# Opening of a two-layer diffusion backbone: filters of both layers in pairs, tokens in two-tile loads, low operands last

## The reference

```
per layer:
  ada = silu(cond) @ w_ada + b_ada          -> sh1, sc1, g1, sh2, sc2, g2
  h   = x * (1 + sc1) + sh1
  z   = h @ w_in                            (1024 x 2816: Hyena, Conformer, q, k, v)
  Hyena filter, for each length L in (1024, 256), from weights alone:
    feats = [t, cos, -sin]                  (L x 33)
    hid = sin(freq * (feats @ w1 + b1)); hid = sin(freq * (hid @ w2 + b2))
    hf  = hid @ w3                          (L x 512: forward and backward half)
    h_fwd, h_bwd = halves of hf * exp(-t * deltas); h_bwd[0] is left out
  ... long convolution, short convolutions, differential attention, w_out,
  layer norms, squared-ReLU MLP
```

## Time and profile before

| | |
|---|---|
| median of three runs | 3832.4 us |
| the profiled execution | 3824.12 us |
| its span in the trace | 3821.4 us |
| mean granted TensorE clock | 0.958 |
| TensorE busy | 3494.9 us (91%) |
| VectorE busy | 1929.1 us (50%) |
| GpSimd busy | 1331.9 us (35%) |
| ScalarE busy | 1100.9 us (29%) |
| mean DMA rate | 97 GB/s |

### The profile page before, as it was taken

The page is one execution under the profiler, slowest core; times in us unless marked ns, Lnnn a source line. Parts: engine busy times, 40 slices in busy tenths (PEclk is TensorE's granted clock), DMA queues, the critical chain, the costliest instruction groups (busy, mean ns, idle before and its releaser), DMA issues. The chain is left out here.

```text
span 3821.4 us, 48345 instructions
## 1 busy us (share of the span) xinstructions
PE 3494.9 (91%) x18386; PEld 2917.0 (76%) x18386; DVE 1929.1 (50%) x2799; ACT 1100.9 (29%) x2020; POOL 1331.9 (35%) x682
## 2 busy tenths in 40 slices
PE   7799997888999999999989999789898999999996
PEld 3577775777778888888867777678687888888885
DVE  3027653876743443344471684387674443344447
ACT  2211243674341111111143113367624111111114
POOL 1445744301253232323363574340025232323222
PEclk7899998999999999999999999899999999999998
DMA  6466645642011111111015774563201111111101
GB/s 238 180 223 220 200 156 165 136 119 81 12 45 45 34 45 34 35 44 37 30 52 201 237 215 160 169 153 101 87 23 45 34 45 34 39 39 35 43 23 55
DMA packets 285239, 369.52 MB, mean 97 GB/s; under 512 B 17111, under 2 KB 202181, under 8 KB 283750
## 3 DMA queue, kind: packets, MB, share of 16 engines
q1 hardware_dynamic: 211826, 212.63, 19.2%
q10 hardware_dynamic: 73204, 153.88, 11.8%
HBM read 276.53 MB, written 81.53 MB: 94 GB/s over the span
## 5 line engine op out<-in xcount | busy, mean ns | idle before, releaser
L768 POOL TENSOR_TENSOR RH<-RAW,ONE 128x1024 fp32r<-128x1024 f32 x200 | 388.4, 1942 | 1498.7 <-PE PS L927 684.7
L927 PE MATMUL PS<-HH,RH 128*128 128x512 f32 (+1 forms) x2752 | 621.9, 370 | 75.3 <-POOL RL L772 27.3
L772 POOL TENSOR_TENSOR RL<-RAW,RH 128x1024 fp32r<-128x1024 f32 x240 | 576.5, 2405 | 162.1 <-ACT RH L1885 146.3
L927 PEld LDWEIGHTS PS<-HH,RH 128*128 128x128 f32 x2752 | 475.4, 196 | 195.7 <-issue 91.8
L927 PE MATMUL PS<-HL,RH 128*128 128x512 f32 (+1 forms) x2752 | 588.5, 357 | 0.0
L927 PE MATMUL PS<-HH,RL 128*128 128x512 f32 (+1 forms) x2752 | 581.4, 354 | 0.0
L2529 DVE SCALAR_TENSOR_TENSOR XT<-PS,ADA,XT 128x512 f32<-128x512 f32 (+1 forms) x704 | 454.1, 663 | 243.9 <-PE PS L1400 240.3
L927 PEld LDWEIGHTS PS<-HL,RH 128*128 128x128 f32 x2752 | 469.6, 192 | 75.4
L927 PEld LDWEIGHTS PS<-HH,RL 128*128 128x128 f32 x2752 | 462.7, 189 | 71.3
L2060 ACT ACTIVATE RB<-PS 128x512 f32<-128x512 f32 (+1 forms) x192 | 101.0, 526 | 1390.4 <-PE PS L927 1390.4
L2513 DVE TENSOR_TENSOR PS<-PS,RB 128x512 f32<-128x512 f32 (+1 forms) x192 | 117.2, 610 | 745.6 <-ACT RB L2060 745.6
(11 more groups left out here) (257 smaller groups left out, 4531.1 us busy)
## 6 DMA issues: line engine op xcount, KB each, us to landing
RAW<-in_w_mlp_dram SPq DMA_DIRECT2D x128, 512.0 KB, 3.9
ADW<-in_w_ada_dram ACTq DMA_DIRECT2D x80, 512.0 KB, 5.9
RAW<-const_dram SPq DMA_DIRECT2D x52, 512.0 KB, 4.1
RAW<-in_w_in_dram SPq DMA_DIRECT2D x44, 512.0 KB, 4.8
z_scratch<-ZST ACTq DMA_DIRECT2D x40, 256.0 KB, 2.8
x_scratch<-XT SPq DMA_DIRECT2D x4, 2560.0 KB, 12.8
QH<-q_hi SPq DMA_DIRECT2D x32, 320.0 KB, 9.3
QL<-q_lo SPq DMA_DIRECT2D x32, 320.0 KB, 10.4
```

The costliest lines, as they stand in the source:

```text
L768: nc.gpsimd.tensor_tensor(RH[:, s, :], RAW[:, p, :], ONE[:].broadcast_to([128, 1024]), ALU.mult)\
L772: nc.gpsimd.tensor_tensor(RL[:, s, :], RAW[:, p, :], RH[:, s, :].bitcast(F32), ALU.subtract)\
L927: mm = pe.matmul(out, w[:, s, k * 128:(k + 1) * 128], m(k), start=(n == 0 and k == 0), stop=(n == 2 and k == KT - 1))
```

## The change

The filter tiles of both layers are made in pairs: `filter_pair(n)` issues the products of tile F_ORDER[n] for layer 0 in array rows 0 to 63 and for layer 1 in rows 64 to 127, into two neighbouring banks (4 and 5, or 6 and 7), and one VectorE operation multiplies both with the decay. The first-token tiles (0 and 8) come first. `FOUT` has four places of twice the size, and one store takes a pair. `DEC` holds only the forward half of the decay table, `DECB` the backward half of the two first-token tiles. TensorE makes four pairs behind the token tiles 6 to 9, one behind each of the second and third modulation products, and four behind the turns, which now go to bank 0. VectorE makes six pairs before the modulation vector and four behind it.

The places in SBUF change: `XIN` goes behind the modulation weights and holds two pairs of token tiles; `HID2` and the two small weights lie below the ring; `FEAT` and `HID1` lie in the first two slots of the high and of the low ring and `ARG` in `RAW`, which all are free after the second sine; `HW3`, `HWS`, the decay and `FOUT` lie in ring slots 2 to 5. So the blocks 0 and 1 are loaded once the second sine is made, ahead of all filter stores, and split before the low parts of the first inputs.

SyncE's order is now: token pairs, blocks 0 and 1, ten filter stores, small vectors, block 2 and so on. The first z product takes high x high by feature tile as these come, then low weights x high inputs, and low inputs last; `vectors()` follows tile 1. The loads of the modulation weights stand earlier among ScalarE's work. The diff, with the changes of mere placement in SBUF and blank lines left out:

```diff
+F_ORDER = (0, ST, *range(1, ST), *range(ST + 1, TT))
...
+    XIN = place("XIN", [128, 2, 2, 1024], F32, WS + OWN * KT * 2048)
...
+    DEC = st.take("DEC", [128, TT, 256])
+    DECB = st.take("DECB", [128, 2, 256])
+    FOUT = place("FOUT", [128, 4, 2, 512], F32, RING_O + RING * 4096 + 8192)
...
-            for t in range(TT):
-                if t >= 2:
-                    sp.wait_ge(x_turned.sem, t - 1)
-                src = x_sample[0, t * 128:(t + 1) * 128, :] if t < ST else \
-                    x_prompt[0, (t - ST) * 128:(t - ST + 1) * 128, :]
-                sp.dma_start(XIN[:, t % 2], src).then_inc(x_in[t % 2].sem, 16)
+            for i in range(TT // 2):
+                if i >= 2:
+                    sp.wait_ge(x_turned.sem, 2 * i - 2)
+                src = x_sample[0, 256 * i:256 * i + 256, :] if i < ST // 2 else x_prompt[0]
+                sp.dma_start(XIN[:, i % 2], src.rearrange("(t p) n -> p t n", p=128)).then_inc(x_in[i % 2].sem, 16)
...
-            def store_filters(l):
-                for t in range(TT):
-                    u = TT * l + t
-                    sp.wait_ge(fout_ready.sem, u + 1)
-                    sp.dma_start(filt_d[l, t], FOUT[:, u % 4].rearrange("p a n -> p (a n)")).then_inc(fout_stored[u % 4].sem, 16)
-            store_filters(0)
-            layer_vectors(0)
+            sp.wait_ge(hf_sin.sem, 2)
             for n in range(2):
                 load_block(0, B_IN + n, column_block(w_in, 0, COLUMNS[n]), True)
-            store_filters(1)
+            for n, t in enumerate(F_ORDER):
+                sp.wait_ge(fout_ready.sem, n + 1)
+                sp.dma_start(filt_d[:, t].rearrange("l p n -> p l n"), FOUT[:, n % 4]).then_inc(fout_stored[n % 4].sem, 16)
+            layer_vectors(0)
...
-            low_of_h(0, 0, KT)
-            for stored in fout_stored:
-                pool.wait_ge(stored.sem, 16 * (DEPTH * TT // 4))
             split(0, B_IN)
             split(0, B_IN + 1)
+            low_of_h(0, 0, KT)
+            for p, stored in enumerate(fout_stored):
+                pool.wait_ge(stored.sem, 16 * len(range(p, TT, 4)))
...
-            def filter_tile(u):
-                l, t = u // TT, u % TT
-                own = slice(64 * l, 64 * l + 64)
-                if u == 0:
+            def filter_pair(n):
+                t, bank = F_ORDER[n], 4 + 2 * (n % 2)
+                if n == 0:
                     pe.wait_ge(hf_sin.sem, 2)
-                if u > 1:
-                    pe.wait_ge(fout_ready.sem, u - 1)
-                pe.matmul(PS[:, 4 + u % 2, :], HID2[own, t * 128:(t + 1) * 128],
-                          (HW3 if t in FIRST_TOKEN else HWS)[own, :],
-                          start=True, stop=True, tile_position=(64 * l, 0)).then_inc(hft_psum.sem, 1)
+                if n > 1:
+                    pe.wait_ge(fout_ready.sem, n - 1)
+                for l in range(DEPTH):
+                    own = slice(64 * l, 64 * l + 64)
+                    pe.matmul(PS[:, bank + l, :], HID2[own, t * 128:(t + 1) * 128],
+                              (HW3 if t in FIRST_TOKEN else HWS)[own, :],
+                              start=True, stop=True, tile_position=(64 * l, 0)).then_inc(hft_psum.sem, 1)
...
-                pe.wait_ge(x_in[t % 2].sem, 16 * (t // 2 + 1))
+                if t % 2 == 0:
+                    pe.wait_ge(x_in[t // 2 % 2].sem, 16 * (t // 4 + 1))
...
+            def ada_turn(rows, col, bank=7):
                 for i in range(4):
-                    mm = pe.matmul(PS[:, 7, col + 2 * i:col + 2 * i + 2], rows[:, 128 * i:128 * i + 128], SEL,
+                    mm = pe.matmul(PS[:, bank, col + 2 * i:col + 2 * i + 2], rows[:, 128 * i:128 * i + 128], SEL,
...
-                if t > 4:
-                    filter_tile(t - 5)
+                if t > 5:
+                    filter_pair(t - 6)
             for b in range(OWN):
                 own_rows(b)
-                filter_tile(5 + b)
+                if b in (1, 2):
+                    filter_pair(b + 3)
             for b in range(OWN):
                 pe.wait_ge(ada_kept.sem, b + 1)
-                ada_turn(AROWS[:, b], 8 * b).then_inc(ada_turned.sem, 1)
-            for u in range(9, DEPTH * TT):
-                filter_tile(u)
+                ada_turn(AROWS[:, b], 8 * b, 0).then_inc(ada_turned.sem, 1)
+            for n in range(6, TT):
+                filter_pair(n)
...
+                def first_product(out):
+                    for n, (w, x) in enumerate(((RH, HH), (RL, HH), (RH, HL))):
+                        for k in range(KT):
+                            if n == 0:
+                                pe.wait_ge(hh_ready.sem, k + 1)
+                            if n == 2:
+                                pe.wait_ge(h_ready.sem, k + 1)
+                            mm = pe.matmul(out, w[:, 0, k * 128:(k + 1) * 128], x[:, k, 0:512],
+                                           start=(n == 0 and k == 0), stop=(n == 2 and k == KT - 1))
+                    return mm
                 def z_tile(at, n, q):
                     t0, tn = CHUNKS[q]
                     weights_ready(l, B_IN + n)
-                    if n == 0:
+                    if n == 0 and (l or q):
                         pe.wait_ge(h_ready.sem, h_ready.at(l, 8 * (q - 2)))
                     if at == 0 and l:
                         pe.wait_ge(m2_evac.sem, m2_evac.at(l - 1, 24 * GROUPS))
                     if at == 0 and l == 0:
-                        pe.wait_ge(fout_ready.sem, TT * DEPTH)
+                        pe.wait_ge(fout_ready.sem, TT)
                     pe.wait_ge(z_evac.sem, z_evac.at(l, at - 3))
-                    mm = column_product(PS[:, 2 + at % 4, 0:tn], slot(l, B_IN + n), lambda k: HH[:, k, t0:t0 + tn],
-                                        lambda k: HL[:, k, t0:t0 + tn])
+                    if at == 0 and l == 0:
+                        mm = first_product(PS[:, 2, 0:tn])
+                    else:
+                        mm = column_product(PS[:, 2 + at % 4, 0:tn], slot(l, B_IN + n), lambda k: HH[:, k, t0:t0 + tn],
+                                            lambda k: HL[:, k, t0:t0 + tn])
                     if q < 2:
                         mm.then_inc(z_psum.sem, 1)
                     else:
                         mm.then_inc(blk_used.sem, 1)
                     if l and at in (1, 2):
                         norm_sums(l - 1, 1, at, (0, 6)[at - 1])
-                    if at == (Z_FIRST - 1 if l else 0):
+                    if at == (Z_FIRST - 1 if l else 1):
...
-            act.dma_start(DEC[:], decay_d.rearrange("(t p) n -> p t n", p=128)).then_inc(decay_in.sem, 16)
+            decay = decay_d.rearrange("(t p) n -> p t n", p=128)
+            act.dma_start(DEC[:], decay[:, :, 0:256]).then_inc(decay_in.sem, 16)
+            act.dma_start(DECB[:], decay[:, 0:ST + 1:ST, 256:512]).then_inc(decay_in.sem, 16)
...
-                if b == 0:
-                    act.wait_ge(x_turned.sem, TT)
...
             place_x(0)
+            load_own(1)
             place_x(1)
             sine(0)
-            load_own(1)
+            load_own(2)
             place_x(2)
             place_x(3)
+            load_own(3)
             sine(1)
-            load_own(2)
             for t in range(4, TT):
                 place_x(t)
-                if t == 5:
-                    load_own(3)
...
-            def filter(u):
-                t = u % TT
-                dve.wait_ge(hft_psum.sem, u + 1)
-                if u == 0:
-                    dve.wait_ge(decay_in.sem, 16)
-                if u > 3:
-                    dve.wait_ge(fout_stored[u % 4].sem, 16 * (u // 4))
+            def filters(n):
+                t, bank = F_ORDER[n], 4 + 2 * (n % 2)
+                dve.wait_ge(hft_psum.sem, 2 * n + 2)
+                if n == 0:
+                    dve.wait_ge(decay_in.sem, 32)
+                if n > 3:
+                    dve.wait_ge(fout_stored[n % 4].sem, 16 * (n // 4))
+                made, out, own = PS[:, bank:bank + 2, :], FOUT[:, n % 4], DEC[:, t:t + 1, :]
                 if t in FIRST_TOKEN:
-                    C.link(V.tensor_tensor(FB[:], PS[:, 4 + u % 2, :], DEC[:, t, :], ALU.mult))
-                    C.link(V.tensor_tensor(FOUT[:, u % 4, 0, :], FB[:, 0:256], FB[:, 256:512], ALU.add))
-                    V.tensor_tensor(FOUT[:, u % 4, 1, :], FB[:, 0:256], FB[:, 256:512], ALU.subtract)\
-                     .then_inc(fout_ready.sem, 1)
+                    dve.wait_ge(fout_ready.sem, n)
+                    back = DECB[:, t // ST:t // ST + 1, :]
+                    for a, d in ((0, own), (256, back)):
+                        C.link(V.tensor_tensor(FB[:, :, a:a + 256], made[:, :, a:a + 256], d.broadcast_to([128, 2, 256]),
+                                               ALU.mult))
+                    C.link(V.tensor_tensor(out[:, :, 0:256], FB[:, :, 0:256], FB[:, :, 256:512], ALU.add))
```

(24 more changed lines are left out.)

13 lines of the change are left out of this document (2 added, 11 removed).

## The result

The kernel after takes 3798.1 us (median of four runs, 3795.2 to 3803.7) against 3831.3 of the kernel before in the same session (four runs): ratio 0.9915 with a 95% interval of 0.9901 to 0.9929, so 33 us less. The forecast was 3807 with 3797 to 3820. The profiled execution took 3796.4 us, its span is 3794.4, 27.0 shorter than that of before.

A forecast was written before the change was run, and what follows sets the result against it. Only the opening, where TensorE waits for low weights and GpSimd for the last filter store, could pay: 0.7 us from an earlier C plus 24.4 from C to Z, 25.1 off the median 3832.4, gives 3807 us, range 3797 to 3820.

The forecast's parts named there:

- Z: Instant where ScalarE evacuates z tile 0 of layer 0: forecast 88.1 us, 113.18 before, 25.1 earlier.
- O: Start of the first product with modulation weights: forecast 55 us, ends 50 and 58; 53.72 before.
- C: Instant where ScalarE starts on the first modulated input: forecast 70.6 us, 71.28 before.
- one-to-one shift: From z tile 0 on: an earlier evacuation passes undiminished to the kernel's end, 25.1 us.
- if tokens were never late: Bound for the first modulation product, from TensorE's own order of transposes and filter pairs alone: about 50.9 us.
- Tokens early, clock up: Rival: token pairs land in about 7.6 us, tile 0 runs at 2.4 GHz; gain 31, 3801 us; chance 0.20.
- O to C: First modulation product to first modulated input: two filter steps of 1.0 us leave, 17.6 becomes 15.6 us.
- C to Z: First modulated input to evacuation of z tile 0: 17.5 us where 41.9 were, worth 24.4 us.
- hidden beside transposes: First-token filter pairs, before the first modulation product: about 2.8 us each, taken to cost nothing.
- The front stays late: Rival: store 0 or last token pair lands late, gain 17.5, 3815 us; with serial filter pairs (3817), chance 0.22.
- blocked splits: Rival: GpSimd's early splits delay low parts if block 1 lands beyond 69, at 104 giving 3842 us; chance 0.04.
- shift given back: Rival: blocks 2 to 5 come late behind the vector loads, gain falls to 6, 3826 us; chance 0.06.

The follow-up runs named there:

- single_loads: The changed kernel with ten token loads of 512 KB, two in flight, instead of five of 1 MB: 3800.9 us, ratio 0.9927 to the kernel before.
- serial_pairs: The changed kernel with the second product of each filter pair waiting for the first: 3821.3 us, ratio 0.9981 to the kernel before.
- own_late: The changed kernel with the modulation weight loads asked for where the kernel before had them: 3795.8 us, ratio 0.9918 to the kernel before.
- blocks_behind: The changed kernel with blocks 0 and 1 loaded behind the last filter store, not ahead of the first: 3812.7 us, ratio 0.9958 to the kernel before.
- the first pair of traces: The first profiled executions of the kernel before and the changed kernel, nothing else altered: spans 27.0 us apart, the changed one 3794.4 us.
- before_queue: The kernel before with only SyncE's order changed, blocks 0 and 1 asked for ahead of all filter stores, small vectors behind: 3824.3 us, ratio 0.9991.
- after_again: The changed kernel run once more, unchanged, for a second trace: 3794.5 us, ratio 0.9905 to the kernel before.
- both of the last versions: The changed kernel with blocks 2 and 3 loaded and split earlier (3790.4 us), and that with the next modulation weights' first load asked for earlier (3785.2 us).

## Why the prediction was right, and where its sum was off

- **The place and the sign.** All of the gain is there at Z, 4.6 us of the 31.7 already at O and 8.3 at C, and it is handed on: tile 2 starts 11.07 behind Z (before 11.04), tile 5 44.86 behind it (45.71). The one-to-one shift held.
- **C was mis-sized.** The forecast took 0.7 us here, 8.3 came. Two steps ahead of O failed. The first is the landing of the pairs: 1 MB at 125 GB/s, 10.6 us, put the last landing at 47.6 and O at 55. The fourth pair came as forecast (38.11), but the last, asked for at 31.99 while the fourth was in flight, landed in 10.0 us at 42.0, only 4 behind the fourth and not 9.6, and from 38.11 on TensorE ran its own order to 49.12. The second is the clock: a transposed tile was taken at 1.97 us and a pair at 2.07, but most of these ran at 2.4 GHz (1.09 and 1.13; the window from 45 us on has 1.00, where before had 0.50). At the forecast's prices the four tiles and four pairs from 38.11 on would take 16.2 us, by my estimate, and put O at 54.3; they took 11.0. So the earlier landing alone would have brought under 1 us, and in single_loads, where the last tile is turned from 49.38 on, nearly as late as in before (49.82), O is still 52.73. Why the clock was up there in after, and not in serial_pairs with TensorE as busy, stays open. That O came near the bound "if tokens were never late", 50.9, is luck: TensorE did wait 6.16 us for the fourth pair, and the clock gave back more than that lost against the bound. The outcome is near the rival "Tokens early, clock up" (O 51, C 66.5, gain 31, 3801), with a chance of 0.20, which came nearer than the likeliest case, though not by its mechanism: the higher clock that it expected in tile 0 came ahead of O instead, while behind the first pass the passes of tile 0 took 3.61 and 3.00 us, with a granted clock of 0.50 from 75 to 80 us. The rule of the Trainium skill that I set beside the sum (turns by packet, tokens half of 392) points the right way. Measured for SyncE's queue, weight blocks included, is 42% with pairs and 29% with single tiles, and pairs landed in 8.5 and 10.0 us, not 7.6. The size of the loads is worth 3.6 us at O (single_loads).
- **O to C** took 13.86, not 15.6. The first modulation block too ran at 2.4 GHz (3.64 for the first two together, where the first alone took 3.06), which is 1.2 us, and the turn took 3.73 and not 4.07. No step had this.
- **C to Z** took 18.5, forecast 17.5, before 41.9. The pairs start together (serial_pairs), no VectorE wait on a store is left, the low parts end 2.7 us before they are wanted (forecast 3), and VectorE's 128x1024 took 1.23 (taken 1.3). The high inputs, not the weights, set the first pass, as forecast.
- **Cost at nothing, wrongly.** The first-token pairs were taken as "hidden beside transposes", but in serial_pairs, where the products of a pair run one behind the other, O comes 14.6 us later. The two row halves working together was worth twice the 10 us that the prediction's rival had, nearly all of it ahead of C, where the rival had 2. And the loads of the modulation weights, moved ahead, cost 3.0 us (own_late).
- **The front stays late; blocked splits; shift given back.** Block 0 was there at 50.7 (the forecast 56), store 0 in time for pair 4 (53.89, no wait). blocks_behind shows what blocked splits cost, 18.2 where the rule of the prediction (1 us of cover, then one for one) gives 18.6. The shift was not given back in the first tiles; the 8 us of the first pair of traces were chance.
- **The sum in time.** A gain of 25.1 was forecast at Z; 31.7 and 35.6 came, with medians 33 and 35 apart. So the opening holds all of it that these runs can tell. Of the forecast's error of 8.9 us in the median 7.6 is that of C (70.6, came 62.98); C to Z erred by 1.0 the other way. The other 2.3 us are less than the runs of one kernel differ by.
- **How near it was.** C, the first product (69.27) and Z (81.48) all lie ahead of the stretches that the prediction named (67 to 74, 76 to 82, 84 to 92), and so does the sixth tile (126.34, not 134). The median lies inside the range by 1.1 us, and that of after_again, 3794.5, lies below it. The mechanism from C on was right, that ahead of C was not, and that the number stayed in the range is in part luck.

Undone one at a time, Z slips by 20.8 (row pairs), 18.2 (early blocks), 6.9 (splits first), 3.8 (token pairs) and 1.5 (low last), and is 3.0 earlier for the loads. That is 48 net, more than the 31.7 won: the edits lean on each other, since each start waits for the last of several things. before_queue shows the other side, where one of them alone gave 7 at Z. What the doubled VectorE operation (1.23 for two filter tiles, 0.69 each before), the fewer stores and the new order of the pairs give by themselves wasn't tried.

## What to carry to other kernels

Follow two or three instants through the opening (here O, C, Z) and give each edit its microseconds at one of them; the end moves with the last. Where two queues shared full DMA engines here, the one with more bytes in flight moved more (42% against 29%), and a load asked for early took from what was needed first. When one wait is taken away, look at once for the next load in line: both of the last versions turned the wait for GpSimd into a wait for weights.

## What the runs showed of the hardware that was not expected

- A VectorE operation between GpSimd's back-to-back ones took 0.94 us in some executions and 6.4 in others of the same kernel, worth 8 us behind it. Two traces are compared only after such a place has been looked for.
- Two 64-row products of 512 columns, one in each row half, took 2.08 us (1.2 GHz) or 1.13 (2.4 GHz) side by side, and 4.20 or 2.30 one behind the other.
- The issue of the small load of `DECB` kept ScalarE's queue for 5.72 us (10.03 to 15.75), behind two large ones, so that the first `place_x` came at 17.20. Why it took so long wasn't tried.

```profile
9.41 0.59 ACTq L1505 DMA_DIRECT2D DEC<-const_dram  x1
10.03 5.72 ACTq L1506 DMA_DIRECT2D DECB<-const_dram  x1
```
